# First loads on one queue, the last two expert tiles bank by bank with their own layer norm, buffers at multiples of 64 bytes

## The reference

```
proj  = x @ w_in                                   # q, k, v, latents, rotary key, gates
y_a   = dilated window attention(q, k, v) @ a_w_out
y_b   = latent attention(c_q, c_kv, k_rope) @ mla_w_out
h     = LN(alpha*x + (g_a*y_a + g_b*y_b) @ w_out; g1, b1)
q     = h @ w_query; top 16 of 128 x 128 product keys in each of 8 heads
y_p   = sum over chosen experts of gate * gelu(h . u_e) * v_e
out   = LN(alpha*h + y_p; ln2_g, ln2_b)
LN(z) = (z - mean(z)) * rsqrt(var(z) + 1e-5) * g + b, over the 2048 channels
```

## Time and profile before

| | |
|---|---|
| median of 3 runs | 2613.54 us (2612.14 to 2613.85) |
| the profiled execution | 2613.9 us |
| its span, first to last instruction | 2612.2 us |
| PE busy | 2551.5 us, 98% |
| DVE, ACT, POOL busy | 56%, 44%, 21% |
| PEclk granted, mean | 0.989 |
| DMA | 521.08 MB, mean 199 GB/s |

### The profile page before, as it was taken

The page is one execution under the profiler, slowest core; times in us unless marked ns, Lnnn a source line. Parts: engine busy times, 40 slices in busy tenths (PEclk is TensorE's granted clock), DMA queues, the critical chain, the costliest instruction groups (busy, mean ns, idle before and its releaser), DMA issues.

```text
span 2612.2 us, 49794 instructions
## 1 busy us (share of the span) xinstructions
PE 2551.5 (98%) x17964; PEld 2384.3 (91%) x17964; DVE 1467.2 (56%) x2383; ACT 1160.4 (44%) x1614; POOL 554.4 (21%) x385
## 2 busy tenths in 40 slices
PE   7999999999999998999999999999999999999995
PEld 7999999999999997999999999999888888888884
DVE  4554554546566655479897434444455555555555
ACT  4444444444444434365554334344444444444443
POOL 0000000000000002048888888600000000000001
PEclk9999999999999998999999999999999999999998
DMA  6666665454445553557787878866677666667672
GB/s 237 214 202 215 213 215 186 162 176 146 143 145 161 187 183 131 183 161 199 191 212 206 202 205 205 236 212 203 217 235 235 229 232 234 234 234 237 235 234 96
DMA packets 179837, 521.08 MB, mean 199 GB/s; under 512 B 52768, under 2 KB 52768, under 8 KB 179536
## 3 DMA queue, kind: packets, MB, share of 16 engines
q1 hardware_dynamic: 123552, 447.80, 52.7%
q0 software_dynamic: 51056, 53.87, 9.6%
q10 hardware_dynamic: 5184, 18.88, 1.8%
HBM read 484.68 MB, written 35.78 MB: 199 GB/s over the span
## 4 chain that ended last, share of the span: by engine, by line
PE 91%; DVE 5%; issue 2%; DMA 1%; ACT 1%; POOL 0%; DVEq 0%; ACTq 0%; POOLq 0%
PE ps L953 60%; PE ps L1149 27%; DVE w_lo L597 1%; PE ps L992 1%; PE ps L994 1%; PE ps L1007 1%; DMA res<-x_t 0%; PE ps L1000 0%; PE ps L1103 0%; PE ps L1118 0%; PE ps L1008 0%; PE ps L987 0%; DVE idx L810 0%; DVE a_lo L776 0%; DMA cst<-const_in 0%
## 5 line engine op out<-in xcount | busy, mean ns | idle before, releaser
L597 DVE TENSOR_TENSOR w_lo<-raw,w_hi 128x1024 fp32r<-128x1024 f32 x850 | 1014.8, 1223 | 856.5 <-ACT w_hi L345 841.2
L953 PE MATMUL ps<-a_hi,w_hi 128*128 128x256 f32 x3984 | 1144.4, 287 | 28.0 <-DVE w_lo L597 23.3
L953 PE MATMUL ps<-a_lo,w_hi 128*128 128x256 f32 x3984 | 1133.3, 284 | 0.0
L953 PE MATMUL ps<-a_hi,w_lo 128*128 128x256 f32 x3984 | 1133.2, 284 | 0.0
L345 ACT ACTIVATE w_hi<-raw 128x1024 fp32r<-128x1024 f32 x850 | 866.2, 1053 | 274.8 <-PE ps L1149 191.6
L953 PEld LDWEIGHTS ps<-a_hi,w_hi 128*128 128x128 f32 x3984 | 770.3, 193 | 34.1 <-issue 22.2
L953 PEld LDWEIGHTS ps<-a_lo,w_hi 128*128 128x128 f32 x3984 | 771.1, 194 | 0.5
L953 PEld LDWEIGHTS ps<-a_hi,w_lo 128*128 128x128 f32 x3984 | 770.5, 193 | 0.0
L308 POOL DMA_INDIRECT g_dram<-gate_v,where x256 | 455.7, 1780 | 199.1 <-DVE gate_v L847 118.6
L1149 PE MATMUL ps<-w_hi,m_hi 128*128 128x512 f32 x1024 | 322.0, 395 | 0.0
L1149 PE MATMUL ps<-w_hi,m_lo 128*128 128x512 f32 x1024 | 321.8, 395 | 0.0
(11 more groups left out here) (161 smaller groups left out, 1691.8 us busy)
## 6 DMA issues: line engine op xcount, KB each, us to landing
raw<-stream SPq DMA_DIRECT2D x850, 512.0 KB
g_dram<-blank POOLq DMA_DIRECT2D x32, 512.0 KB, 6.1
a_dram<-act ACTq DMA_DIRECT2D x32, 512.0 KB
a_in<-a_dram POOLq DMA_DIRECT2D x32, 512.0 KB, 5.1
g_in<-g_dram POOLq DMA_DIRECT2D x32, 512.0 KB, 6.3
g_dram<-gate_v,where POOLq DMA_INDIRECT x256
res<-x_t ACTq DMA_DIRECT2D x4, 512.0 KB, 8.7
ln_s<-ln POOLq DMA_DIRECT2D x1, 2048.0 KB, 11.1
```

The costliest lines, as they stand in the source:

```text
L597: dve.tensor_tensor(w_lo[:, s, :], raw[:, s, :], w_hi[:, s, :].bitcast(F32), ALU.subtract).then_inc(lo_ready, 1)
L953: ins = pe.matmul(out, w, a, start=first and q == 0, stop=last and q == 2)
```

## The change

SP issues the quarters of x itself, among the first four halves; ACT no longer issues them. The waits for `par_in` and `par_in2` stand later in `head_a(0)`: on ACT before the gate's bias is added, on VectorE ahead of the first softmax. TensorE's loop over the second expert product ends before the last eight tiles; six follow written out, and the last two are done bank by bank. The end of the kernel is new: the residual gives the row sums (`accum_out`), ACT squares the centred values with `accum_out`, and VectorE multiplies by g before the root is known and adds b after it, into a second array `u_s`. GpSimd has no part in it. The sizes of `cst`, `small` and `carrier` are raised to multiples of 16 floats, and `blank` moves behind them.

```diff
 C_TOKEN = C_SLOPE + HEADS
-N_CONST = C_TOKEN + TT
+N_CONST = C_TOKEN + 16
 S_BG, S_QN, S_KN, S_G1, S_B1 = 0, 2 * KD, 2 * KD + KL, 2 * KD + 2 * KL, 3 * KD + 2 * KL
-N_SMALL = 4 * KD + 2 * KL
+N_SMALL = 4 * KD + 2 * KL + 8
...
     stat = sb("stat", [P, 16])
-    carrier = sb("carrier", [P, 1])
-    blank = sb("blank", [P, T])
+    carrier = sb("carrier", [P, 16])
...
     mean_s = sb("mean_s", [P, T], F32, mix_mem)
...
-    bn = sb("bn", [P, TT, 4, 6], F32, up_mem)
-    bn2 = sb("bn2", [P, TT, 2], F32, up_mem)
+    u_s = sb("u_s", [P, TT, D], F32, up_mem)
+    sums = sb("sums", [P, TT, 4], F32, up_mem)
+    squares_s = sb("squares_s", [P, TT, 4], F32, up_mem)
+    moment = sb("moment", [P, TT, 4], F32, up_mem)
+    junk = sb("junk", [P, 4, 512], F32, up_mem)
     up_mem.close()
...
     m_ready, mhi_ready, mlo_ready, y_ready = sem("m_ready"), sem("mhi_ready"), sem("mlo_ready"), sem("y_ready")
...
-        with sp.Fori(0, N_TILES // 2) as i:
+        def x_part(q):
+            sp.dma_start(res[:, 4 * q:4 * q + 4, :], x_t[:, 4 * q:4 * q + 4, :]).then_inc(x_in[q], 16)
+        for s in range(2):
+            x_part(2 * s)
+            sp.dma_start(raw[:, s, :], stream[s]).then_inc(raw_in[s], 16)
+            x_part(2 * s + 1)
+        for s in range(2, 4):
+            sp.wait_ge(lo_ready, s + 1)
+            sp.dma_start(raw[:, s, :], stream[s]).then_inc(raw_in[s], 16)
+        with sp.Fori(1, N_TILES // 2) as i:
             for s in range(4):
...
                 sp.wait_ge(out_ready, 4 * tt + c + 1)
-                sp.dma_start(y_out[tt][:, o], y_s[:, tt, o]).then_inc(y_done, 16)
+                sp.dma_start(y_out[tt][:, o], u_s[:, tt, o]).then_inc(y_done, 16)
         sp.wait_ge(y_done, 16 * 4 * TT)
...
-        pool.wait_ge(ln2_in, 16)
-        for tt in range(TT):
-            for c in range(4):
-                o = slice(512 * c, 512 * c + 512)
-                pool.wait_ge(g_ready, 4 * tt + c + 1)
-                pool.tensor_tensor(y_s[:, tt, o], y_s[:, tt, o], ln2_s[:, 1, o], ALU.add).then_inc(out_ready, 1)
     def _(act):
-        for q in range(4):
-            act.dma_start(res[:, 4 * q:4 * q + 4, :], x_t[:, 4 * q:4 * q + 4, :]).then_inc(x_in[q], 16)
         for b in range(2):
...
                 hi(Tile(0), (q // 2,))
-        act.wait_ge(par_in, 16)
...
             exps(h, False)
+            if first:
+                act.wait_ge(par_in, 16)
             done(t)
...
         for tt in range(TT):
-            act.wait_ge(mv_ready, tt + 1)
-            act.activation(stat[:, 6 + tt:7 + tt], bn2[:, tt, 1:2], ACT.Sqrt, bias=stat[:, 14:15]).then_inc(sd_ready, 1)
-            act.wait_ge(nb_ready, tt + 1)
+            act.wait_ge(nmean_ready, tt + 1)
             for c in range(4):
...
+                act.activation(junk[:, c, :], y_s[:, tt, 512 * c:512 * c + 512], ACT.Square, bias=moment[:, tt, 0:1],
+                               accum_out=squares_s[:, tt, c:c + 1]).then_inc(act_step, 1)
+            act.wait_ge(act_step, 5 * tt + 4)
+            act.activation(junk[:, 0, 0:4], squares_s[:, tt, :], ACT.Identity, accum_out=moment[:, tt, 1:2]).then_inc(act_step, 1)
+            act.wait_ge(act_step, 5 * tt + 5)
+            act.activation(moment[:, tt, 2:3], moment[:, tt, 1:2], ACT.Sqrt, bias=stat[:, 14:15], scale=1.0 / D).then_inc(sd_ready, 1)
...
                 lo(Tile(0), (q // 2,))
-        dve.wait_ge(par_in, 16)
-        dve.wait_ge(par_in2, 16)
...
             lo(t.next())
+            if first:
+                dve.wait_ge(par_in, 16)
+                dve.wait_ge(par_in2, 16)
             softmax(h, True, h)
...
-            dve.memset(carrier[:], 0.0)
+            dve.memset(carrier[:, 0:1], 0.0)
...
-        def inverse(tt):
+        def residual(tt, c):
+            o = slice(512 * c, 512 * c + 512)
+            dve.wait_ge(y_ready, 4 * tt + c + 1)
+            return dve.scalar_tensor_tensor(out=y_s[:, tt, o], in0=h1_n[:, tt, o], scalar=ALPHA,
+                                            in1=ps[:, D * tt + 512 * c:D * tt + 512 * c + 512], op0=ALU.mult, op1=ALU.add,
+                                            accum_out=sums[:, tt, c:c + 1])
+        def mean(tt, ins):
+            link(ins)
+            link(dve.tensor_reduce(moment[:, tt, 1:2], sums[:, tt, :], AX_X, ALU.add, negate=True))
+            link(dve.tensor_scalar(moment[:, tt, 0:1], moment[:, tt, 1:2], 1.0 / D, None, ALU.mult))
+            dve.sem_inc(nmean_ready, 1)
+        def times_g(tt, c):
+            o = slice(512 * c, 512 * c + 512)
+            return dve.scalar_tensor_tensor(out=u_s[:, tt, o], in0=y_s[:, tt, o], scalar=moment[:, tt, 0:1], in1=ln2_s[:, 0, o],
+                                            op0=ALU.add, op1=ALU.mult)
+        def inverse(tt, ins):
+            link(ins)
             dve.wait_ge(sd_ready, tt + 1)
...
+            link(dve.reciprocal(moment[:, tt, 3:4], moment[:, tt, 2:3]))
+        def plus_b(tt, c):
+            o = slice(512 * c, 512 * c + 512)
+            dve.scalar_tensor_tensor(out=u_s[:, tt, o], in0=u_s[:, tt, o], scalar=moment[:, tt, 3:4], in1=ln2_s[:, 1, o],
+                                     op0=ALU.mult, op1=ALU.add).then_inc(out_ready, 1)
         dve.wait_ge(ln2_in, 16)
...
+        for c in range(4):
+            ins = residual(0, c)
+        mean(0, ins)
+        times_g(0, 0)
+        times_g(0, 1)
+        residual(1, 0)
+        times_g(0, 2)
+        ins = times_g(0, 3)
+        residual(1, 1)
+        inverse(0, residual(1, 2))
+        for c in range(2):
+            plus_b(0, c)
+        mean(1, residual(1, 3))
+        for c in range(2, 4):
+            plus_b(0, c)
+        for c in range(4):
+            ins = times_g(1, c)
+        inverse(1, ins)
+        for c in range(4):
+            plus_b(1, c)
...
-        with pe.Fori(0, NKEYS // 8) as i:
+        def up_bank(t, b, tt, c):
+            s = slice(P * tt, P * tt + P)
+            o = D * tt + 512 * c
+            w = slice(512 * (c % 2), 512 * (c % 2) + 512)
+            pe.matmul(ps[:, o:o + 512], m_hi[:, b % 2, s], w_hi[:, t.slot(c // 2), w], start=False, stop=False, skip_group_check=True)
+            pe.matmul(ps[:, o:o + 512], m_hi[:, b % 2, s], w_lo[:, t.slot(c // 2), w], start=False, stop=False, skip_group_check=True)
+            return pe.matmul(ps[:, o:o + 512], m_lo[:, b % 2, s], w_hi[:, t.slot(c // 2), w], start=False, stop=False,
+                             skip_group_check=True)
+        with pe.Fori(0, NKEYS // 8 - 1) as i:
             for b in range(8):
                 up(Tile(T_UP + b, i, 8), i * 8 + b, b)
+        for b in range(6):
+            up(Tile(T_UP + NKEYS - 8 + b), NKEYS - 8 + b, b)
+        last = (Tile(N_TILES - 2), Tile(N_TILES - 1))
+        for b, t in enumerate(last):
+            pe.wait_ge(mlo_ready, NKEYS - 1 + b)
+            for c in range(4):
+                if c % 2 == 0:
+                    half_ready(t, c // 2)
+                ins = up_bank(t, b, 0, c)
+                if b == 1:
+                    ins.then_inc(y_ready, 1)
+        for c in range(4):
+            up_bank(last[0], 0, 1, c)
+            up_bank(last[1], 1, 1, c).then_inc(y_ready, 1)
...
         "small_in": np.ascontiguousarray(np.concatenate([
-            v[n].reshape(-1, P) for n in ("b_gates", "mla_q_norm", "mla_kv_norm", "ln1_g", "ln1_b")]).T),
+            v[n].reshape(-1, P) for n in ("b_gates", "mla_q_norm", "mla_kv_norm", "ln1_g", "ln1_b")] + [
+            np.zeros((8, P), np.float32)]).T),
         "keys_t": np.ascontiguousarray(np.stack([v["peer_sub_keys_1"].T, v["peer_sub_keys_2"].T], axis=1)),
```

More of the change, by code:

```diff
@@ L166, in build @@
     mean_s = sb("mean_s", [P, T], F32, mix_mem)
+    blank = sb("blank", [P, T], F32, mix_mem)
     mix_mem.close()
@@ L230, in build @@
     m_ready, mhi_ready, mlo_ready, y_ready = sem("m_ready"), sem("mhi_ready"), sem("mlo_ready"), sem("y_ready")
-    g_ready = sem("g_ready")
-    z_ready, mv_ready, sd_ready, nb_ready, ln_ready, out_ready, y_done = (
-        sem("z_ready"), sem("mv_ready"), sem("sd_ready"), sem("nb_ready"), sem("ln_ready"), sem("out_ready"), sem("y_done"))
+    z_ready, nmean_ready, sd_ready, out_ready, y_done = (
+        sem("z_ready"), sem("nmean_ready"), sem("sd_ready"), sem("out_ready"), sem("y_done"))
     dve_step, act_step = sem("dve_step"), sem("act_step")
@@ L574, in _ @@
         for tt in range(TT):
-            act.wait_ge(mv_ready, tt + 1)
-            act.activation(stat[:, 6 + tt:7 + tt], bn2[:, tt, 1:2], ACT.Sqrt, bias=stat[:, 14:15]).then_inc(sd_ready, 1)
-            act.wait_ge(nb_ready, tt + 1)
+            act.wait_ge(nmean_ready, tt + 1)
             for c in range(4):
-                o = slice(512 * c, 512 * c + 512)
-                act.activation(y_s[:, tt, o], y_s[:, tt, o], ACT.Identity, bias=stat[:, 10 + tt:11 + tt],
-                               scale=stat[:, 8 + tt:9 + tt]).then_inc(ln_ready, 1)
+                act.activation(junk[:, c, :], y_s[:, tt, 512 * c:512 * c + 512], ACT.Square, bias=moment[:, tt, 0:1],
```

(6 more changed lines are left out.)

## The result

The changed kernel takes 2590.6 us, the median of four runs (2590.37 to 2591.99), against 2612.84 for the kernel before in the same series. The ratio is 0.9916, with a 95% interval of 0.9904 to 0.9929: 22 us less, between 18.5 and 25. The forecast was 2593.6 in a range of 2589.5 to 2598.5. Run once more beside other kernels it gave 2590.87.

A forecast was written before the change was run, and what follows sets the result against it. TensorE's matmuls bound the kernel (91% of the chain); only its waits at start and end could be won. 7.4 + 12.5 + 0 = 19.9 us off the median 2613.54 gave 2593.6, range 2589.5 to 2598.5.

The forecast's parts named there:

- The wait for the constants: Start: VectorE's wait on par_in2 holds tile 1's differences; tile 1 begins 6.0 us earlier, plus 1.4 us of low clock.
- The rate of one queue: First loads, all on SP's queue: 339 GB/s, 1.55 us a transfer, against 414 GB/s with two queues.
- the first rival: First loads: one queue is as fast as two, the start gains 8.4 us, total 2592.6; chance 0.14.
- part 1: First loads: x on SP's queue and the waits moved later; 7.4 us less, bounds 5.0 to 9.0.
- The constants behind the first loads: Start: constants issued after q3 land by about 22, first use past 28 us, raw3 has a margin; no stall.
- TensorE's new stall: Last two tiles: TensorE waits 1.1 us for m_lo of tile 127, costing nothing of its own.
- VectorE's line and ACT's squares: End: VectorE never idle from 2581.9, 0.69 us per times g or plus b, squares 0.80; 12.5 us less.
- The buffer sizes: Buffers moved to multiples of 64 bytes: zero effect, bounds 3 us gained to 3 us lost.
- another matmul pace in the middle: Sign of being wrong: matmuls in the middle change pace, where the expert product was to stay at 233 ns.
- The fourth rival: Second expert product: new addresses slow TensorE's reads; at 4%, 9.3 ns a matmul, 28.7 us, total 2622; chance 0.02.
- Code fetch: TensorE's new loop exit before the last eight tiles: fetching code costs 4.23 us, total 2597.8; chance 0.07.
- worse end: End: dearer squares or table loads, VectorE waits 2 to 3.5 us for the second root, total 2596.5; chance 0.10.

The follow-up runs named there:

- e5: Kernel before with only the two waits moved, x still on ACT's queue; 2605.26 us, ratio 0.9971.
- e12: Changed kernel with x on ACT's queue again, so two queues at the start; 2591.49 us, ratio 0.9918.
- e9: Changed kernel with the gated activations of tile 127 made ahead of the second half of its weights; 2591.41 us, ratio 0.992.
- e7: Kernel before with the last two tiles bank by bank but the old layer norm; 2615.14 us, ratio 1.0007.
- e10: Changed kernel with carrier 24 floats long, so every buffer behind it begins 32 bytes off a multiple of 64; 2598.4 us, ratio 0.9945.
- e4: Changed kernel without the new buffer sizes; 2592.63 us, ratio 0.992.
- e1: Kernel before with x on SP's queue and both waits moved, nothing else; 2605.61 us, ratio 0.997.
- e11: The changed kernel once more, unaltered, beside the others on one chip; 2590.87 us, ratio 0.9919.

## Why the prediction held, step by step

- **The wait for the constants.** Right. It was the cause of the gap; without it the second stretch at the low clock goes too, and e5 shows that the waits alone give about 6.5 us.
- **The rate of one queue, the first rival.** This term was mis-sized. I took 339 GB/s, measured 401; raw2's copy starts at 13.56 where I had it landed at 14.5, tile 0 runs without a gap, and tile 1 begins at 16.40, not 17.0. So it was the mechanism of the first rival that came true, with its 8.4 us for part 1. That the mean of the traces, 7.7, lies nearer to the forecast's 7.4 is in part luck: part 1 gave 8.15 us in the one trace, 6.9 in the other (36.23 - 29.36), and the number of slow matmuls after the first (14 and 28 in these two) alone moves it by 1.3 us. The Trainium skill, "DMA: Bandwidth & Descriptors", section "Issuing engines are not separate DMA queues", says that issuing from several engines at once saves only the sequencer's time; here one queue moves 401 GB/s and two 415 (e12, the same window), so the traces of this case agree within 4%.
- **The constants behind the first loads.** Right: no stall before tile 3.
- **TensorE's new stall.** Right in place and size: 1.1 forecast, 0.9 of waiting and 1.16 to 1.18 in the end interval (e9, e7). I wrote that it costs nothing of its own, since VectorE is never idle from 2581.9 on. That was wrong. VectorE's closed line starts when the first bank is ready, so a later first bank moves the whole line; e9 gets 1.16 us back, all of it. The sum held the stall all the same, since it lets the residuals begin at bank times behind it.
- **VectorE's line and ACT's squares.** Right: 0.69 for times g and plus b (2.73 and 2.74 us for four), squares every 0.70 us, read of the sum included, not 0.80, no table load. From the last piece to the end it is 3.07 us, where I took 2.75 as before. From the start of tile 126 to the end 25.7 us, 26.0 by my sum: 12.9 us less instead of 12.5; 13.1 us from the last matmul to the end, 13.5 forecast.
- **The buffer sizes.** The zero was wrong, by 1.0 us, inside the bounds of 3 us; another matmul pace in the middle was among my signs of being wrong, and it came. I had compared 284 ns in a_lo with 281 in b_lo and seen no loss, but aligned buffers were then 279. The two rows differ for another reason than the address, and I had none with the address alone changed. The fourth rival, slower reads at new addresses, didn't occur here, but e10 shows that it exists: an offset of 32 bytes costs 7.5 us. (The constants and `small` grow by 88 bytes a partition, 22 floats, not the 24 bytes that I gave.)
- **Code fetch, worse end.** Neither occurred.

The sum: 8.15 + 12.9 + 1.0 is 22.05, against 21.9 between the profiled spans and 19.9 forecast; each of the three terms was too small. What is left is scatter in the stages between. The first expert product takes 596.2 us in two traces (before, e5) and 595.0 in the others, and that gave 1.2; the stretch between the mixing products and it took 281.3 to 283.6 us in the fourteen traces, and between these two it took 1.3 back. Why these stages scatter stays open.

## What to carry to other kernels

On an in-order engine look at what stands behind a wait, not only at what needs it: moving the waits behind work that doesn't need them gave about 6.5 us, and the order of the loads 0.7. A last stage is shortened by two changes that are worth more together: let the producer finish its outputs one after the other, and give the consumer pieces that need only one of them; alone the first cost 1.2 us and the second gave 6.5, together 12.9. Where an engine's line is closed up to the end, its start time is the end time, so a small stall ahead of it counts in full.

## What the runs showed of the hardware

TensorE's pace depends on where its operands lie in SBUF. Against offset 0, offset 44 costs 0.6 ns on each of the 768 matmuls with b_hi or b_lo in the mixing products (0.43 us), and offset 32 costs 2.2 ns (1.70 us) there and 1 ns in the second expert product. The moving operand counts (b_hi and b_lo in the mixing products), and at offset 32 also the stationary one, since in the second expert product m_hi and m_lo are the only operands of TensorE that moved. Counted from a multiple of 64 bytes (by the declared sizes), offset 0 gave 178.66, offset 44 gave 179.09 and offset 32 gave 180.36 us for the same mixing products. That 32 is worse than 44 is not explained; whether 32 itself counts or the address in a larger unit stays open, since only three addresses were tried, and between before and after the arrays also moved by 876 bytes in all.

After its first matmul TensorE gave 13 to 28 matmuls at the slow pace in six kernels whose starts are alike (e4 13, the changed kernel 14, e1 18, e10 22, e9 24, e11 28), which moves the start by up to 1.4 us (15 x 0.093). What sets the number was not tested.
